# Modulation product with the weights as the stationary side, and conv's weights loaded earlier in each round of the front

## The reference, cut to what matters

```python
c_act = jax.nn.silu(c)
mod = c_act @ w_ada[l] + b_ada[l]                 # (1,2048) @ (2048, 12288)
sh_a, sc_a, gt_a, sh_f, sc_f, gt_f = split(mod, 6)
h = _rmsnorm(x, norm_mix[l]) * (1.0 + sc_a) + sh_a
p = h @ w_in[l]                                   # split into cq, ckv, k_pe, q, k, v, z, b, a, gates
```

## Time and profile before

| | |
|---|---|
| median of 3 runs | 2295.18 us (2292.54 to 2296.31) |
| profiled execution | 2293.58 us, span in the trace 2292.3 us |
| PE busy | 2235.2 us, 98% of the span |
| DVE, ACT busy | 1505.7 us (66%), 1009.0 us (44%) |
| DMA | 506.75 MB, mean 221 GB/s |
| first two of 40 slices (57 us each) | 363 and 381 GB/s, then 240, 209, ... |

### The profile page before, as it was taken

One profiled execution on the slowest core, in us unless ns is written; L12 is line 12 of the kernel. 1 busy time (PEld: TensorE's weight loads), 2 busy tenths in 40 slices (PEclk: granted clock), 3 DMA queues, 4 the chain that ended last, 5 costly groups with the idle time before them and its releaser, 6 DMA issues.

```text
span 2292.3 us, 26935 instructions
## 1 busy us (share of the span) xinstructions
PE 2235.2 (98%) x10767; PEld 1855.7 (81%) x10767; DVE 1505.7 (66%) x1927; ACT 1009.0 (44%) x1270; POOL 24.4 (1%) x28
## 2 busy tenths in 40 slices
PE   5998999999999999999999999999999999999998
PEld 3678898888887888888888888887888888888886
DVE  5888898887768777765554555467555555555556
ACT  4345445343444464443344434456444444434444
POOL 0000000000000000000000000000000000000000
PEclk9999999999999999999999999999999999999999
DMA  9966767685678768876555565555555555555553
GB/s 363 381 240 209 245 228 258 198 271 197 220 269 307 275 239 285 273 242 202 184 192 193 184 202 184 191 195 193 191 195 188 188 188 190 187 185 194 197 189 130
DMA packets 276445, 506.75 MB, mean 221 GB/s; under 512 B 24032, under 2 KB 38112, under 8 KB 275296
## 3 DMA queue, kind: packets, MB, share of 16 engines
q1 hardware_dynamic: 276320, 505.03, 65.0%
HBM read 502.51 MB, written 2.49 MB: 220 GB/s over the span
## 4 chain that ended last, share of the span: by engine, by line
PE 82%; DVE 8%; DMA 4%; ACT 2%; issue 2%; SPq 0%; POOL 0%; DVEq 0%; ACTq 0%
PE bank L1200 25%; PE bank L1202 25%; PE bank L1201 25%; DVE WL L1927 3%; PE bank L1391 2%; DMA RAW<-in_w_o_dram 2%; DVE GA L1908 1%; PE bank L1121 1%; ACT WH L1480 1%; PE bank L1212 1%; PE bank L1214 1%; PE bank L1213 1%; DMA RAW<-in_w_o_gdn_dram 1%; PE bank L1148 1%; PE bank L1363 1%
## 5 line engine op out<-in xcount | busy, mean ns | idle before, releaser
L1927 DVE TENSOR_TENSOR WL<-RAW,WH 128x1024 fp32r<-128x1024 f32 (+1 forms) x714 | 864.9, 1218 | 619.2 <-ACT WH L1480 616.5
L1480 ACT CAST WH<-RAW 128x1024 fp32r<-128x1024 f32 (+1 forms) x714 | 743.3, 1047 | 917.6 <-PE bank L1202 733.1
L1200 PE MATMUL bank<-WH,HTh 128*128 128x512 f32 x1936 | 770.4, 398 | 7.3 <-DVE WL L1927 6.5
L1202 PE MATMUL bank<-WH,HTl 128*128 128x512 f32 x1936 | 755.9, 390 | 0.0
L1201 PE MATMUL bank<-WL,HTh 128*128 128x512 f32 x1936 | 755.5, 390 | 0.0
L1200 PEld LDWEIGHTS bank<-WH,HTh 128*128 128x128 f32 x1936 | 364.2, 188 | 88.7 <-DVE WL L1927 11.3
L1201 PEld LDWEIGHTS bank<-WL,HTh 128*128 128x128 f32 x1936 | 364.4, 188 | 77.1 <-issue 4.3
L1202 PEld LDWEIGHTS bank<-WH,HTl 128*128 128x128 f32 x1936 | 364.0, 188 | 76.5
L1908 DVE SCALAR_TENSOR_TENSOR GA<-RAW,ST,GA 128x512 f32<-128x512 f32 x264 | 181.2, 747 | 13.9 <-DMA RAW<-in_w_ada_dram 7.7
L1200 PE MATMUL bank<-WH,R2h 128*128 128x512 f32 x408 | 164.1, 402 | 3.5 <-DVE WL L1927 3.5
L1202 PE MATMUL bank<-WH,R2l 128*128 128x512 f32 x408 | 159.9, 392 | 0.0
(11 more groups left out here) (273 smaller groups left out, 1756.3 us busy)
## 6 DMA issues: line engine op xcount, KB each, us to landing
RAW<-in_a_w_in_dram SPq DMA_DIRECT2D x96, 1024.0 KB, 5.0
RAW<-in_w_gate_up_dram SPq DMA_DIRECT2D x88, 1024.0 KB, 5.0
RAW<-in_w_ada_dram SPq DMA_DIRECT2D x80, 1024.0 KB, 5.2
RAW<-in_w_in_dram SPq DMA_DIRECT2D x63, 1024.0 KB, 5.0
RAW<-in_w_down_dram SPq DMA_DIRECT2D x44, 1024.0 KB, 5.0
RAW<-in_a_w_out_dram SPq DMA_DIRECT2D x32, 1024.0 KB, 5.0
A<-in_w_ada_dram SPq DMA_DIRECT2D x16, 1024.0 KB, 11.7
RAW<-in_w_o_dram SPq DMA_DIRECT2D x16, 1024.0 KB, 5.1
```

The source lines that it names most:

```text
L1200: e.matmul(o, ah[:, s], hi[:, k, :], start=first, stop=False)
L1202: i = e.matmul(o, al[:, s], hi[:, k, :], start=False, stop=last)
L1480: e.copy(hi, rv).then_inc(S["hi"], 1)
L1927: e.tensor_tensor(lo, rv, hi.bitcast(F32), ALU.subtract).then_inc(S["lo"], 1)
```

## The change

Two things. First, for chunks 0 to 7 the product has its sides swapped: GA and the fourth unit are loaded as weights, 128x128 at a time, and one column moves (of ones, or of `c_act`). 6 matmuls become 24. The result comes in columns: 4 columns for GA and 4 for the fourth unit, and DVE adds bias and both in two operations on 4 columns. The multiply by the identity, the reduction, and the buffers `CB` and `JX` go. Second, the load order of a round and the steps with it: ckv's and conv's weights move ahead, so that conv's stand in front of the last three units of the second chunk, and the conv halves in front of its product.

```diff
@@ mod_value
-    return 3 * ci + 3 if ci < 8 else 24 + ci - 7
+    return 2 * ci + 2 if ci < 8 else 16 + ci - 7
@@ Schedule.plan_units
-            u.extend([w[0]] + f[:1] + [w[1]] + f[1:5] + [w[2]] + f[5:] + [w[3]])
+            u.extend([w[0]] + f[:1] + [w[1]] + f[1:3] + [w[2]] + f[3:5] + [w[3]] + f[5:])
@@ Schedule.front
             for j in (jobs[0], jobs[1]):
                 self.front_halves(j, where[j.name])
-            for _ in range(4 * more):
+            for _ in range(2 * more):
                 self.front_unit()
             self.front_unit()
             self.front_halves(jobs[2], where[jobs[2].name])
-            if more:
-                self.front_unit()
-                self.front_unit()
-                self.put("mod_e", 2 * c + 2, None)
-                self.put("cam", c + 1)
+            for _ in range(2 * more):
                 self.front_unit()
             self.front_unit()
             if more:
-                self.front_unit()
+                self.put("mod_e", 2 * c + 2, None)
+                self.put("cam", c + 1)
             else:
                 self.put("rope_tables")
             self.front_halves(jobs[3], where[jobs[3].name])
+            for _ in range(4 * more):
+                self.front_unit()
@@ pe_program, step mod
-                for h in range(2):
-                    e.matmul(b, ones, L.GA[:, ci % 2, h, :], start=h == 0, stop=False)
-                W.wait_ge("cact", 3)
+                for m in range(4):
+                    for h in range(2):
+                        e.matmul(b[:, m:m + 1], L.GA[:, ci % 2, h, m * P:(m + 1) * P], ones[:, 0:1],
+                                 start=h == 0, stop=h == 1)
+                W.wait_ge("cact", 2)
                 W.wait_ge(f"raw{sch.raw_slot(i)}", sch.raw_value[i])
-                for t in range(4):
-                    i = e.matmul(b, L.CB[:, t, :], rv[:, t, :], start=False, stop=t == 3)
+                for m in range(4):
+                    for t in range(4):
+                        i = e.matmul(b[:, 4 + m:5 + m], rv[:, t, m * P:(m + 1) * P], L.cact[:, 12 + t:13 + t],
+                                     start=t == 0, stop=t == 3)
@@ dve_program, step begin
-            W.wait_ge("cact", 2)
-            e.tensor_copy(L.CB, bc4(L.cact[:, 12:16])).then_inc(S["cact"], 1)
@@ dve_program, step mod_e
-                b = bank[4 if ci == 1 else 5].rearrange("p (j n) -> p j n", n=P)
-                W.wait_ge("mod", 3 * ci)
-                e.tensor_tensor(L.JX, b, bm4(L.ident), ALU.mult).then_inc(S["mod"], 1)
-                W.wait_ge("mod", 3 * ci + 1)
-                e.tensor_reduce(L.craw[:, 0:4], L.JX, AX, ALU.add).then_inc(S["mod"], 1)
-                W.wait_ge("mod", 3 * ci + 2)
-                new = L.craw[:, 0:4]
+                b, part = bank[4 if ci == 1 else 5], L.craw[:, 0:4]
+                W.wait_ge("mod", 2 * ci)
+                e.tensor_tensor(part, b[:, 4:8], COL[:, j0:j0 + 4], ALU.add).then_inc(S["mod"], 1)
+                W.wait_ge("mod", 2 * ci + 1)
+                e.tensor_tensor(L.MOD[:, j0:j0 + 4], b[:, 0:4], part, ALU.add).then_inc(S["mod"], 1)
+                continue
```

More of the change, by code:

```diff
@@ L233, in __init__ @@
         self.XT0 = by_head(64, 4096)
-        self.CB = ar(57, 512).rearrange("p (t n) -> p t n", n=P)
-        self.JX = ar(97, 512).rearrange("p (j n) -> p j n", n=P)
         self.tmp1 = [ar(32, 1024), ar(36, 1024)]
```

## The result

| | before | after |
|---|---|---|
| median | 2294.52 us (4 runs) | 2329.99 us (4 runs, 2326.82 to 2334.61) |
| profiled execution, span | 2293.58, 2292.3 us | 2327.96, 2326.7 us |
| mean granted clock of PE | 0.996 | 0.981 |

What follows compares the result with a forecast made beforehand. The DMA sets the front's 30.4 us round, with PE 1.8 us short of full. Longer PE rounds give +11 us and three clock falls +5.1, total +16.3: 2311.5 us on the 2295.18 median, own range 2307 to 2316, wider 2302 to 2338.

Steps and rivals of the forecast that it cites:

- I take it that a PE that is never idle keeps its clock: One-column products: PE issuing without pause stays at full clock, as in the 128-column transposes; 5.34 us a product.
- The second rival: One-column products count as idle for the clock, half speed in the front's products: +24 us on top, 2335.5 us; chance 0.24.
- the clock at the new holes: One fall of PE's clock at each of three new holes before sm, 1.7 us each, +5.1 us.
- a record of 0.11 us at full speed: One-column products on PE: 48 load and matmul records at 0.111 us, 5.34 us a product, +0.12 each.
- the eviction: DVE between product and h: two operations on 4 columns take 0.46 us instead of 1.71, -1.25 us.
- the hole before sm: PE idle from the second product's end to sm: 0.2 to DVE, 0.46 eviction, 2.1 to sm's first matmul.
- the way from product to cq: PE from second product to next cq: 6.3 us behind a 5.34 us product, 5.15 in the last round.
- conv and its wait: Conv halves on PE, 5.75 us, plus 0.5 us waiting per round while DVE finishes eight accumulations.
- a warm round of 34.2: PE's round, cq to cq, at full clock in the new order: 34.2 us twice, 33.1 the last.
- The order's share with a full clock: Whole front without clock falls: three rounds 103.2 against 91.1 us, less 1.1 at the start, so +11 us.
- the clock holds at the holes: First rival: no clock fall at the new holes before sm, so +11 only, 2306 us; chance 0.17.
- products are cheap enough to leave the DMA in front: Third rival: products below 3.45 us, 0.072 a record, so the DMA sets the round: 2292.5 us; chance 0.07.

Runs made afterwards that it cites:

- 64 columns, first wide: Changed kernel in the new load order, 64 columns moving instead of one, chunk 0 with the old wide product and eviction: 2313.07 against 2295.79 us, 1.0077.
- columns-alone run: One-column products and short eviction of the changed kernel, in the load order of before: 2321.49 us, 1.0125 against the kernel before.
- filled: The new-order kernel with 64 columns and wide chunk 0, plus 12 unread 256-column matmuls in each of three holes before sm: 2312.61 us, 1.0074 against before.
- with ckv's split moved ahead: New-order kernel with 64 columns and wide chunk 0, no filler matmuls, ckv's weights loaded and split right behind cq's: 2307.52 us, 1.0057 against before.
- the filled kernel with ckv's split ahead: New-order kernel with 64 columns, wide chunk 0 and filler matmuls in the holes, ckv's weights loaded and split right behind cq's: 2308.67 against 2294.39 us, 1.0059.

## Why the prediction was wrong, step by step

PE in the front, in us from start to start: the forecast (the first cq and those behind a hole with its +1.7 each), the kernel with 64 columns and a wide first product, and the changed kernel; three rounds each.

| piece | forecast | 64 columns, first wide | changed kernel |
|---|---|---|---|
| first cq starts | 46.04 | 46.38 | 50.46 |
| cq + ckv | 12.7 | 13.15, 13.75, 13.15 | 13.80, 13.15, 13.53 |
| first product | 5.34 | 5.27, 5.27, 5.27 | 7.93, 5.79, 5.28 |
| conv and the wait | 6.25 | 6.15, 6.15, 6.15 | 7.88, 8.35, 7.33 |
| second product to sm | 8.1 | 8.19, 8.18, 8.19 | 9.55, 9.00, 10.00 |
| sm to cq | 3.5, last 2.4 | 3.52, 3.51, 2.29 | 3.51, 3.51, 2.62 |
| fourth cq starts | 152.6 | 154.57 | 171.69 |

**The step that failed** is "I take it that a PE that is never idle keeps its clock". It was carried over from the 128-column transposes to products of one column, which no row covered. The columns-alone run refutes it: a PE without a pause, a clock of 0.72. The second rival had the mechanism, with a chance of 0.24 against 0.52. Its size: 24 us over the forecast, 17.1 at the fourth cq between the last two columns of the table. The rival's bookkeeping was off in both directions. Up to the first cq it had 8.4 us, and 4.1 came. The first product costs 3.8 where 3.1 was forecast: 2.5 itself and 1.3 in the transposes, which begin slow too (31.99 to 38.23 is 6.2 us for 5.0). The second, which was to lose 5.3 as wholly slow, loses 0.6: it begins fast, and the way to sm is 8.7 us for 8.1. The six others were to lose 2.6 each, 15.6 in all; with conv behind them they lose 12.3. The first of a round loses 2.66, 0.52 and 0.01, and conv behind it 1.7, 2.2 and 1.2, since the fall comes late in the product and is handed on, which the rival did not count; the second loses 1.4, 0.8 and 1.8 and hands on next to nothing (sm to cq is the same), since the hole behind it drops the clock in either kernel: one fall, not two. The pieces cq + ckv and sm to cq add the last 0.7. Fewer falls at a full price, with part of the price behind them, came to less than the rival's 24.

The Trainium skill's rule that the prediction weighed (TensorE: Matmul & The Clock Gate, Part 4, PE-mode transpose) stays contradicted for the transposes of this kernel (float32): those at full speed kept it, and in the changed kernel PE came out of them faster than it went in (0.106 us a record in the product at 38.23, 0.214 in the one ahead of them). Carried over to one-column matmuls, as the prediction did in a sentence, it gave the side that came true.

**A step that was missing:** the wait of ckv for its split. It follows from the load order that stands ahead of the prediction: `cq | g g | ckv` puts two units of the first chunk, eight accumulations on DVE, between the two splits. The prediction priced the other eight of a round, those of the second chunk behind conv's split, and took cq and ckv as following each other without a wait. With a fast clock it is worth 2.0 us a round (12.85 against 10.89 for cq + ckv, filled, with and without it). In the column "64 columns, first wide" the three pieces of cq + ckv come to 40.05 us for 38.1 forecast, which is nearly all of the 2.0 us by which it ends above the forecast; with ckv's split moved ahead they come to 37.46 (12.84, 13.58, 11.04).

**A term sized too high:** the clock at the new holes, 1.7 each, 5.1 in all. The clock did fall at each. But where ckv waits for DVE the three falls cost 2.4 us, and where it doesn't 3.1. That the kernel with 64 columns and a wide first product came to +17.3, close to the forecast's +16.3, is thus in part two errors against each other: the clock's price too high, ckv's wait left out.

**Right:** a record of 0.11 us at full speed (5.27 and 5.28 a product for 5.34 forecast); the eviction, 0.46; the hole before sm, 2.62 for 2.76; the way from product to cq, 11.7 for 11.64, 10.5 for 10.5 in the last round; conv and its wait, 6.15 for 6.25; a warm round of 34.2, measured as 34.36 once clock and wait are out of the way (some 0.35 of it the filler's); and that what the front loses stays lost (33.45 us at the fourth cq, 34.4 in the span). The order's share with a full clock, forecast at +11, is +14.3 in the filled kernel with ckv's split ahead (fourth cq at 152.48, 14.2 late): of the 3.2 us between, 0.85 is a later first cq, 0.7 the first cq and ckv (13.38 for 12.7), and the filler's 1.9 more than covers the rest.

The rivals that the clock holds at the holes, and that products are cheap enough to leave the DMA in front, are both out: the clock reads 0.50 behind each hole, and no product of 24 matmuls came under 5.27.

## What to carry to other kernels

Swapping sides to get a result in column form trades moved columns for weight loads; at full clock PE's time was the same (5.3 us for 5.2), but with a single moving column PE lost its clock while it issued without a pause. Where a product must be narrow, move copies of the column: here 64 took the same time as one at full clock (5.27 us a product against 5.28) and kept the clock. From a slow start they did not help, and the wide form was the better one. Read PE's busy share and its granted clock together, and price a fall of the clock at the next steps, not at the one that causes it; before filling a hole for the clock's sake, look for the wait that stands right behind it.

## What the runs showed of the hardware that was not expected

- PE busy in 30.00 of 30 us with a mean granted clock of 0.72, with products of 48 one-column records; 1.00 with the same 48 loads and 64 columns each.
- At the start of the program the granted clock reads 1.00 from 20 to 40 us in all these kernels, while records of a first product with 1 or 64 columns take 0.214 us, as later where it reads 0.50. There the lengths tell the level and the column does not.
- From a slow start, a product of 512-column matmuls reached full speed within its 7.0 to 8.3 us; products with 1 or 64 columns (10.3 us) did not, and PE got fast only in the transposes behind them.
- Holes of 2.6 us dropped the clock every time, but for very different lengths: 2.7 us of lost time behind one, 0.15 and 0.22 behind two others, in one kernel, with the clock low for 10.2, 3.4 and 3.4 us.
